# Sums over features as four 32-column products each: two blocks of a language model on one core

## What is computed

```python
def rmsnorm(x, g):
    y = xf * lax.rsqrt(jnp.mean(xf * xf, axis=-1, keepdims=True) + EPS)     # 1024 features of a token

def gated_group_rmsnorm(y, z, g):
    h = h * lax.rsqrt(jnp.mean(h * h, axis=-1, keepdims=True) + EPS)        # 512 features of a group

def layernorm(x, g, b):
    mu = jnp.mean(xf, axis=-1, keepdims=True)
    var = jnp.mean(xc * xc, axis=-1, keepdims=True)

# second block: heads of 64 (queries and keys) and 128 (differential attention) features
qa = apply_rope(rmsnorm_2(qa.reshape(B, S, A_Q_HEADS, HEAD_DIM), qn_a[l]), cos, sin)
ob = rmsnorm_2(ob, subln_b[l]) * (1.0 - lam_init)
```

## Time and profile before

| | us |
|---|---|
| median of three runs | 2560.54 (2560.17 to 2560.57) |
| the profiled execution, as a whole | 2562.39 |
| span in the profile, from the first to the last instruction | 2560.5 |
| TensorE busy (matmul) | 2494.3 |
| TensorE weight loads | 2042.2 |
| VectorE busy | 1264.0 |
| ScalarE busy | 920.8 |
| GpSimd busy | 1045.5 |

### The profile page before, as it was taken

How to read it: one execution, slowest core, us unless ns; L and a number is a source line. 1 busy time by engine, 2 the same in 40 slices (tenths; PEclk the granted TensorE clock), 3 DMA queues, 4 the chain that set the end, 5 groups by cost and what they waited for, 6 DMA issues and landing times.

```text
span 2560.5 us, 29207 instructions
## 1 busy us (share of the span) xinstructions
PE 2494.3 (97%) x11835; PEld 2042.2 (80%) x11835; DVE 1264.0 (49%) x2010; ACT 920.8 (36%) x1527; POOL 1045.5 (41%) x480
## 2 busy tenths in 40 slices
PE   8989998999999999999999999999999999999999
PEld 6778887788887887888888788888777778788887
DVE  7776676554444698464433542223466545422222
ACT  3434443222223386222223232223466642122221
POOL 4334334544444410654444544444222234544442
PEclk9999999999999998999999899999999999999999
DMA  4112222454442200354433233233111123233322
GB/s 155 50 58 73 68 75 66 150 180 164 163 150 91 90 34 9 124 189 164 158 115 99 85 99 99 92 98 99 58 58 58 50 66 99 82 99 99 95 95 91
DMA packets 70982, 252.56 MB, mean 99 GB/s; under 512 B 8000, under 2 KB 8512, under 8 KB 70848
## 3 DMA queue, kind: packets, MB, share of 16 engines
q1 hardware_dynamic: 58752, 210.27, 25.5%
q10 hardware_dynamic: 12096, 40.42, 4.4%
HBM read 248.56 MB, written 2.10 MB: 98 GB/s over the span
## 4 chain that ended last, share of the span: by engine, by line
PE 88%; DVE 8%; ACT 3%; issue 1%; POOL 0%; ACTq 0%; DMA 0%; DVEq 0%; POOLq 0%
PE ps L507 26%; PE ps L508 26%; PE ps L509 26%; PE ps L523 2%; PE ps L547 1%; PE ps L554 1%; DVE XL L1432 1%; PE ps L585 1%; DVE arena L1423 1%; PE ps L738 1%; PE ps L739 1%; PE ps L740 1%; DVE tmpm L1423 1%; PE ps L653 1%; DVE XL L1423 1%
## 5 line engine op out<-in xcount | busy, mean ns | idle before, releaser
L2136 POOL TENSOR_TENSOR WL<-raw,WH 128x1024 fp32r<-128x1024 f32 x391 | 950.9, 2434 | 1250.1 <-ACT WH L926 1243.3
L507 PE MATMUL ps<-XH,WH 128*128 128x512 f32 x3160 | 1249.7, 395 | 33.7 <-DVE XL L1423 15.9
L508 PE MATMUL ps<-XL,WH 128*128 128x512 f32 x3160 | 1237.4, 392 | 0.0
L509 PE MATMUL ps<-XH,WL 128*128 128x512 f32 x3160 | 1236.9, 391 | 0.0
L507 PEld LDWEIGHTS ps<-XH,WH 128*128 128x128 f32 x3160 | 598.1, 189 | 169.0 <-issue 21.7
L509 PEld LDWEIGHTS ps<-XH,WL 128*128 128x128 f32 x3160 | 597.8, 189 | 126.5
L508 PEld LDWEIGHTS ps<-XL,WH 128*128 128x128 f32 x3160 | 598.4, 189 | 124.1 <-issue 2.2
L926 ACT ACTIVATE WH<-raw 128x1024 fp32r<-128x1024 f32 x306 | 322.4, 1057 | 736.4 <-PE ps L509 605.2
L1423 DVE SCALAR_TENSOR_TENSOR arena<-arena,ps 128x512 f32<-128x512 f32 x88 | 60.4, 686 | 519.0 <-ACT arena L1122 506.0
L2134 POOL CAST WH<-raw 128x1024 fp32r<-128x1024 f32 x85 | 95.2, 1120 | 243.4 <-PE ps L509 219.2
L1423 DVE SCALAR_TENSOR_TENSOR h<-ps,der,h 128x512 f32<-128x512 f32 x104 | 77.3, 750 | 160.3 <-PE ps L509 160.1
(11 more groups left out here) (250 smaller groups left out, 1903.3 us busy)
## 6 DMA issues: line engine op xcount, KB each, us to landing
raw<-in_w SPq DMA_DIRECT2D x394, 512.0 KB, 3.7
arena<-in_w_mod ACTq DMA_DIRECT2D x72, 512.0 KB, 4.4
o_out<-h SPq DMA_DIRECT2D x8, 256.0 KB, 2.0
h<-in_x SPq DMA_DIRECT2D x4, 256.0 KB, 8.0
h<-in_x ACTq DMA_DIRECT2D x4, 256.0 KB, 7.2
raw<-in_w SPq DMA_DIRECT2D x2, 256.0 KB, 4.7
arena<-in_c ACTq DMA_DIRECT2D x1, 512.0 KB, 4.3
vec<-in_vec ACTq DMA_DIRECT2D x1, 295.5 KB, 9.7
```

Source lines behind the costliest of these rows:

```text
L507: e.matmul(b, wh, XH[:, x, :], start=i == 0, stop=False)
L508: e.matmul(b, wh, XL[:, x, :], start=False, stop=False)
L509: p = e.matmul(b, wl, XH[:, x, :], start=False, stop=i == len(slots) - 1)
L2136: e.tensor_tensor(lo, x, hi.bitcast(F32), SUB).then_inc(*did(("split", c)))
```

## The change

In `token_sums` each product, which had 128 tokens as its stationary columns, is made as four, with 32 of the columns each. Product q writes to the 32 partitions of the bank that belong to its tokens, so it uses its own quarter of the array's columns. The moving operand is the same. The flags that begin and end a sum in PSUM are given to all four. The semaphore is still raised by the last product of a call only. The change has no other part; all the 53 calls go through it.

```diff
             def token_sums(b, src, mat, start, stop):
+
                 n = mat.shape[1]
                 for c in range(4):
-                    p = e.matmul(b[:, c * n:(c + 1) * n], src[:, c * P:(c + 1) * P], mat, start=start and c == 0,
-                                 stop=stop and c == 3)
+                    for q in range(0, P, 32):
+                        p = e.matmul(b[q:q + 32, c * n:(c + 1) * n], src[:, c * P + q:c * P + q + 32], mat,
+                                     start=start and c == 0, stop=stop and c == 3)
                 return p
```

## The result

| | median, us (range, runs) | kernel before on the same chip, us | ratio with 95% interval |
|---|---|---|---|
| changed kernel | 2537.2 (2534.5 to 2539.8, 4) | 2560.56 | 0.9906 [0.9893, 0.9918] |

The changed kernel takes 23.4 us less by the medians and 24.1 by the ratio, where 16.6 less were forecast. The profiled execution took 2539.79 as a whole, with a span of 2538.0, against 2562.39 and 2560.5: 22.6 less in the trace.

What follows compares the result with a forecast made beforehand. TensorE bounds the kernel, its sums bound by loading weights; 3.9 + 0.9 + 0.6 + 2.4 + 2.0 + 0.8 + 6.0 = 16.6 us less, 2560.5 - 16.6 = 2544 us. Range 2537 to 2566.

Steps and rivals of the forecast that it cites:

- Quarters side by side: All 53 calls: quarters load at once, 0.28 a call instead of 0.90; 16.6 us less in total, chance 0.47.
- The bounds from half-width loads and from the drain: Mixer rows: half-width loads 0.007 and 0.05 to 0.06 apart, 0.09 drain; taken for quarter steps of 0.032 and switches.
- Issue decides: Rival, everywhere: 0.035 us to issue each product, 0.56 a call, only 7.3 us less, 2553; chance 0.26.
- Quarters take turns: Rival, all calls: quarters' matmuls start no closer than 0.03, switches come on top, 9.9 us more, 2570; chance 0.15.
- The keeps: Discounted gains: conformer's other eleven calls 2.0 of 3.6, first layer's group sums 0.8 of 1.3, second mixer 6.0 of 7.1.
- The clock left at nothing: Whole kernel: no gain counted from the granted clock; a fall more or less, 2 to 3 us, went into the range.
- s5 and s6: Two norms whose second call waits for the last square: 0.45 us less each, 0.9 together.
- The conformer's sums: Five calls in a row before the spread at the conformer's end, last one waiting for ScalarE's square: 2.4 us less.
- s4's 0.6: A norm with four calls, where VectorE's L1794 waited 0.59 for the last: 0.6 us less.

Runs made afterwards that it cites:

- e6: Changed kernel with the sixteen quarter products of each call made twice; 3.1 us less than the kernel before, ratio 0.9990.
- e7: Kernel before with the four whole products of each call made twice; 74.0 us more than the kernel before, ratio 1.0291.
- e1: Changed kernel with two halves of 64 columns per product instead of four quarters; 11.9 us less than the kernel before, ratio 0.9945.
- e8: Changed kernel with the sums at the conformer's end drawn together in larger groups; 19.8 us less than the kernel before, ratio 0.9921.
- e4: Quarters only in the conformer's 16 calls, whole products elsewhere; 7.7 us less than the kernel before, ratio 0.9974.
- e3: Quarters only in the second mixer's 17 calls, whole products elsewhere; 7.4 us less than the kernel before, ratio 0.9970.
- e5: Changed kernel with the conformer's last five calls made of whole products again; 20.4 us less than the kernel before, ratio 0.9917.
- e2: Changed kernel with its two loops exchanged, all four products of one quarter first; 2.2 us less than the kernel before, ratio 0.9993.
- e9: Changed kernel plus unread 256-column products in TensorE's waits behind four norms; 32.2 us less than the kernel before, ratio 0.9877.

## Why the prediction was right in its mechanism and short in its size

**Quarters side by side: shown.** Loads 0.007 apart in fours and 0.03 within a quarter, a call of 0.28, a pair of 0.84 where 0.83 was worked out, and a marginal 0.27 (e6) against 0.90 (e7). The bounds from half-width loads and from the drain carried to quarters, and halves (e1) lie between.

**Issue decides: fell** where TensorE had been busy. A pair of 32 products runs at 0.0175 a product (0.56 over 32), half the 0.035 of the earlier trace rows, and e1 with half the products is slower. Longer rows do have stalls, of 0.56 to 2.75 in e6 and e8, for which the profile shows no wait; whether they are this issue isn't shown. The conformer's last five calls in the changed kernel, with waits of 0.64 and 0.23 among them, have none.

**Quarters take turns: fell.** 32 matmul records start within 0.26 in each call, 0.008 apart in the mean, far below 0.03. The Trainium skill's least distance of about 25 ns (TensorE: Matmul & The Clock Gate, section "Wait — 56ns, not 53.3ns?") thus doesn't bind the whole array here; within one quarter, 0.032 is above it. The prediction read a second rule of the Trainium skill as speaking against the change (TensorEngine Tiling (Array Packing), section "Instruction Overhead"). That section advises not to take the tiling factor from a dimension that is already small. Here the factor comes from the 128 stationary columns and not from the one that moves, so that advice isn't put to the test. Sixteen one-column products take 0.28 where four took 0.90: in the earlier trace rows the weight load was what bound them.

**Which terms were too small.** The forecast was 6.4 short against the 23.0 of the table. The steps that failed:
- *The keeps.* I kept 2.0 of 3.6 in the conformer, 0.8 of 1.3 in the group sums and 6.0 of 7.1 in the mixer, as ScalarE or VectorE "set the pace". All of it came: 3.8, 1.4, 6.9, together 3.3 more. These calls stand between products that TensorE had ready; the waits for and behind sums grew nowhere but at s4 to s6 and the conformer's end. A discount needed a wait in the trace at that very place, and the earlier trace rows show waits at other places.
- *The clock left at nothing.* At the conformer's end 2.3 came with it. I had the 0.80 of the earlier trace rows in hand, ahead of the spread, and looked only at the falls behind s4 to s6; of these, s5 and s6 stayed as they were and s4's became 3.4 us shorter. As e4 shows, the 2.3 need not have come: the forecast should have had a term of 0 to 2.3 here.
- *Small ones.* The conformer's sums gave 2.8 instead of 2.4: the last call was done 0.4 after its square (987.40 to 987.82), where I had put 0.6. s5 and s6 gave 0.6 each instead of 0.45, as a call behind a wait went from 0.90 to the quick end of its bounds.

**Right by luck.** s4's 0.6 came, but e3 has 0.56 of it without quarters: the wait of L1794 stood behind two calls at half clock. Of the conformer's sums, too, 1.1 goes with the clock, as e5 shows. With the 2.3 behind the spread some 4 of the 23.0 go with the clock, which the sum of the prediction had at nothing.

**The range** began at 2537, which held full keeps (3.2 below 2544) and one clock fall less (2 to 3). Both came at once, with 0.7 of the small terms on top, for which it had no room: 2536.5 by the ratio, 2537.2 by the median.

## What to carry to other kernels

Products with one or two moving columns were bound here by loading their stationary operand (0.11 us of load against 0.03). Splitting that operand over column quarters, with neighbouring instructions in different quarters, made the loads run side by side, for 0.29 us of switching that is paid per group and not per call. The 0.09 ahead of the group stands in the trace; the other 0.20 is what the sum leaves, and its division into 0.09 and 0.11 isn't shown. Before taking a discount for "another engine may come last", look for a wait at that place in the trace; without one, keep the gain. Where TensorE waits behind a norm, a few products without use can be worth more than the norm's own shortening, if the granted clock falls there: 2.2 against 0.6 at s5.

## What was not expected of the hardware

- Overlap of quarters needs them near each other in the program: with eight records of one quarter in a row, the next quarter's load started 0.15 us after the first one's, when six of the eight had started (e2).
- Long rows of short products have stalls with nothing in the profile that TensorE waits for: none in the changed kernel's five calls of sixteen products, 0.56 in the last of six calls (e8), 0.64 and 2.75 in five calls made twice and 1.61 in s4's four made twice (e6). In e8 waits of 1.14 and 0.23 stood in the same row and didn't prevent it. The cause wasn't looked into.
- With twice as many one-column sums the mean granted clock went from 0.985 to 0.973, at 27 us beyond their own time (e7), though TensorE was busy with them; with eight records of 256 columns in a wait it was 1.00 over s5, where it was 0.81 without (e9).
